# Attention's scores on split operands, keys and queries split in the q stage

## The reference

```python
q = (hn @ w_q).reshape(bsz, L, XATTN_HEADS, XATTN_HEAD_DIM)
k, v = jnp.split(mn @ w_kv, 2, axis=-1)
s = jnp.einsum("blhd,bmhd->bhlm", q, k).astype(jnp.float32) * (XATTN_HEAD_DIM ** -0.5)
p = jax.nn.softmax(s, axis=-1).astype(v.dtype)
o = jnp.einsum("bhlm,bmhd->blhd", p, v).reshape(bsz, L, D_MODEL)
return o @ w_xo
```

## Time and profile before

| | us |
|---|---|
| median of 3 runs | 2433.53 (2432.92 to 2438.96) |
| the profiled execution's own time | 2435.23 |
| its span, first to last instruction | 2433.5 |
| PE (TensorE) busy | 2408.2, 99% |
| PEld (weight loads) busy | 2185.0, 90% |
| DVE (VectorE) busy | 1642.0, 67% |
| ACT (ScalarE) busy | 771.1, 32% |
| POOL (GpSimd) busy | 256.3, 11% |

### The profile page before, as it was taken

How to read it: one execution, slowest core, us unless ns; L and a number is a source line. 1 busy time by engine, 2 the same in 40 slices (tenths; PEclk the granted TensorE clock), 3 DMA queues, 4 the chain that set the end, 5 groups by cost and what they waited for, 6 DMA issues and landing times.

```text
span 2433.5 us, 34372 instructions
## 1 busy us (share of the span) xinstructions
PE 2408.2 (99%) x12524; PEld 2185.0 (90%) x12524; DVE 1642.0 (67%) x3028; ACT 771.1 (32%) x1277; POOL 256.3 (11%) x263
## 2 busy tenths in 40 slices
PE   8999999999999999999999999999999999999998
PEld 6788887788889888888889999999999999999997
DVE  7735453578883884262474687888888788777776
ACT  6401110322223431130352253433333343333333
POOL 0088860000000220000000000001001000000000
PEclk9999999999999999999999999999999999999999
DMA  7532227742227542213332122233232622222222
GB/s 248 162 135 89 77 80 127 209 126 78 73 86 212 207 186 78 95 50 122 114 113 87 44 70 69 83 102 103 91 106 100 257 79 68 76 76 83 76 76 76
DMA packets 121662, 267.25 MB, mean 110 GB/s; under 512 B 15552, under 2 KB 67264, under 8 KB 121536
## 3 DMA queue, kind: packets, MB, share of 16 engines
q1 hardware_dynamic: 113552, 239.85, 31.0%
q0 software_dynamic: 6688, 22.55, 2.5%
q10 hardware_dynamic: 1296, 3.17, 0.4%
HBM read 200.55 MB, written 67.08 MB: 110 GB/s over the span
## 4 chain that ended last, share of the span: by engine, by line
PE 93%; DVE 3%; ACT 1%; DMA 1%; issue 1%; SPq 0%; DVEq 0%; ACTq 0%
PE bank L816 30%; PE bank L818 30%; PE bank L817 30%; PE bank L1062 1%; ACT PB L1570 1%; DVE ON L1827 1%; DVE PT L1827 1%; PE bank L1057 0%; DVE PB L2311 0%; PE bank L1009 0%; DVE smx L2303 0%; PE bank L1016 0%; DMA scratch_KV<-KVS 0%; DMA MEM<-memT 0%; ACT ON L1310 0%
## 5 line engine op out<-in xcount | busy, mean ns | idle before, releaser
L816 PE MATMUL bank<-XN,WLO 128*128 128x512 f32 x1200 | 468.7, 391 | 0.6 <-issue 0.6
L817 PE MATMUL bank<-XN,WHI 128*128 128x512 f32 x1200 | 467.8, 390 | 0.0
L818 PE MATMUL bank<-XN,WHI 128*128 128x512 f32 x1200 | 467.8, 390 | 0.0
L816 PE MATMUL bank<-XH,EL 128*128 128x384 f32 x1232 | 412.8, 335 | 0.0
L817 PE MATMUL bank<-XL,EH 128*128 128x384 f32 x1232 | 412.2, 335 | 0.0
L818 PE MATMUL bank<-XH,EH 128*128 128x384 f32 x1232 | 412.2, 335 | 0.0
L816 PEld LDWEIGHTS bank<-XN,WLO 128*128 128x128 f32 x1200 | 225.4, 188 | 48.8 <-issue 1.8
L817 PEld LDWEIGHTS bank<-XN,WHI 128*128 128x128 f32 x1200 | 225.4, 188 | 47.1 <-issue 0.5
L818 PEld LDWEIGHTS bank<-XN,WHI 128*128 128x128 f32 x1200 | 225.4, 188 | 46.7
L816 PE MATMUL bank<-AF,EL 128*128 128x384 f32 (+2 forms) x704 | 237.0, 337 | 0.5 <-DVE HR L2465 0.3
L817 PE MATMUL bank<-AF,EH 128*128 128x384 f32 (+2 forms) x704 | 235.9, 335 | 0.0
(11 more groups left out here) (295 smaller groups left out, 3760.7 us busy)
## 6 DMA issues: line engine op xcount, KB each, us to landing
RAW<-W_all SPq DMA_DIRECT2D x131, 512.0 KB, 3.6
WR<-W_all SPq DMA_DIRECT2D x92, 512.0 KB, 4.6
scratch_G<-GS SPq DMA_DIRECT2D x16, 768.0 KB, 3.8
scratch_VW<-TB POOLq DMA_DIRECT2D x16, 544.0 KB, 3.4
XS<-xT SPq DMA_DIRECT2D x8, 768.0 KB, 6.0
scratch_CO<-COS SPq DMA_DIRECT2D x8, 768.0 KB, 5.9
COL<-scratch_CO SPq DMA_DIRECT2D x8, 768.0 KB, 4.3
G2L<-scratch_G SPq DMA_DIRECT2D x8, 768.0 KB, 5.8
```

What stands on the lines that cost most here:

```text
L816: pe_mm(out, w[1], x[0], start=first, stop=False, skip_group_check=onto)
L817: pe_mm(out, w[0], x[1], start=False, stop=False, skip_group_check=onto)
L818: return pe_mm(out, w[0], x[0], start=False, stop=last, skip_group_check=onto)
```

## The change

Scores are computed with `product`, from split queries and split keys. The splitting is done once, in the q stage. For each slot j: SyncE loads key tile j (`KF`), ScalarE copies its high part (`KH`), VectorE makes the rest (`KT_LO`), SyncE stores both. Each block of queries goes from PSUM to `QF`, a single buffer (VectorE), to `QH` (ScalarE), to `QT` (VectorE), and SyncE stores both as separate tensors. ScalarE's high part of the next weights (`hi`) stands behind the slot's three copies of queries. In attention the loads of queries and keys are doubled, keys are loaded per head and group. The last slot of the q stage is that of `last_pair`. ScalarE and SyncE wait for all stores of queries before softmax(0) and before `QL` of round 2. The order of work on each engine in a round is as before.

```diff
--- before.py
+++ after.py
@@ -206,18 +206,20 @@
     SQ2 = at("SQ2", 48, [2, T])
     ACC2 = at("ACC2", 82, [T])
     NT = at("NT", 88, [BLK])
-    QS = at("QS", 66, [2, T])
+    QF, QH, QT = at("QF", 64, [BLK]), at("QH", 66, [2, BLK], F32R), at("QT", 70, [2, BLK], F32R)
+    KF, KH, KT_LO = at("KF", 74, [M2]), at("KH", 76, [M2], F32R), at("KT_LO", 78, [M2], F32R)
     XR = at("XR", 66, [2, T])
-    KL = at("KL", 48, [2, 2, M2])
+    KL = at("KL", 48, [2, 2, 2, NMEM], F32R)
     VU = at("VU", 56, [2, 2, 2, 2, P], F32R)
     PB = at("PB", 64, [2, 4, NMEM])
     PT = at("PT", 72, [2, 2, BLK], F32R)
-    QL = at("QL", 80, [2, 2, BLK])
+    QL = [[at("QL00", 80, [2, BLK], F32R), at("QL01", 84, [2, BLK], F32R)], [at("QL10", 88, [2, BLK], F32R)]]
 
     def low(name, kb, shape, dt=F32):
 
         return nc.alloc_sbuf_tensor_at(name, [P] + shape, dt, offset=base + int(kb * K))
 
+    QL[1].append(low("QL11", 18, [2, BLK], F32R))
     YL = low("YL", 0, [HT, C, NC])
     WO += [low(f"WO{q}", S5B_KB[q], [QUAD, 2, P]) for q in range(1, GROUPS // QUAD)]
     ML += [low(f"ML{q}", S5B_KB[q] + 4, [QUAD, P]) for q in range(2, GROUPS // QUAD)]
@@ -253,7 +255,8 @@
     U_d, CO_d, G_d, BB_d, L_d, M_d, Y_d, KV_d, Q_d = (
         scratch[k] for k in ("U", "CO", "G", "BB", "L", "M", "Y", "KV", "Q"))
     W_d = nc.dram_tensor("scratch_VW", (P, GROUPS, 2 * (ROW + GP)), F32).ap()
-    K_d = KV_d[0:KT]
+    K_d = [KV_d[0:KT]] + [nc.dram_tensor(f"scratch_K{n}", (KT, P, M2), F32).ap() for n in range(2)]
+    QQ_d = [Q_d, nc.dram_tensor("scratch_QR", (KT, P, T), F32).ap()]
     VV_d = [v.rearrange("e p (m d) -> e p m d", d=P) for v in
             (KV_d[KT:2 * KT], nc.dram_tensor("scratch_VR", (KT, P, M2), F32).ap())]
 
@@ -576,16 +579,32 @@
         with loop(nc.sync, 3) as i:
             wo(i, True)
         wo(3, False)
-        def queries(i):
-            for par in range(2):
-                weights(SLOT0["q"] + par + 2, par, i)
-                sp.wait_ge(evac, RES0["q"] + NB * (par + 1) + 2 * NB * i)
-                sp.dma_start(tile_of(Q_d, 2 * i + par), QS[:, par, :]).then_inc(S(f"q_stored{par}"), 16)
-
-        def load_memory(h):
-
-            sp.dma_start(KL[:, h % 2], K_d[2 * h:2 * h + 2].rearrange("e p m -> p e m")
-                         ).then_inc(S(f"memory_in{h % 2}"), 16)
+        def keys_load(j):
+
+            sp.dma_start(KF[:], K_d[0][j]).then_inc(S("memory_in0"), 16)
+
+        def keys_store(j):
+
+            sp.wait_ge(S("x_lo"), KT + 4 * j + 1)
+            for to, part in zip(K_d[1:], (KH, KT_LO)):
+                sp.dma_start(to[j], part[:].bitcast(F32)).then_inc(S(f"kv_stored{j % 2}"), 16)
+
+        def queries_store(j):
+
+            for b in range(NB):
+                n = NB * j + b
+                sp.wait_ge(S("x_lo"), KT + 4 * j + b + 2)
+                for to, part in zip(QQ_d, (QH, QT)):
+                    sp.dma_start(to[j][:, blk(b)], part[:, n % 2, :].bitcast(F32)
+                                 ).then_inc(S(f"q_stored{n % 2}"), 16)
+
+        def load_keys(u):
+
+            h, m = u // 2, slice(u % 2 * NMEM, (u % 2 + 1) * NMEM)
+            for part in range(2):
+                sp.dma_start(KL[:, u % 2, part].bitcast(F32),
+                             K_d[1 + part][2 * h:2 * h + 2, :, m].rearrange("e p m -> p e m")
+                             ).then_inc(S(f"memory_in{u % 2}"), 16)
 
         def load_values(u):
 
@@ -597,30 +616,43 @@
 
         def load_queries(n):
             h, b = divmod(n, NB)
-            sp.dma_start(QL[:, n % 2], Q_d[2 * h:2 * h + 2, :, blk(b)].rearrange("e p t -> p e t")
-                         ).then_inc(S(f"queries_in{n % 2}"), 16)
-
-        queries(0)
-
+            for part in range(2):
+                sp.dma_start(QL[n % 2][part][:].bitcast(F32),
+                             QQ_d[part][2 * h:2 * h + 2, :, blk(b)].rearrange("e p t -> p e t")
+                             ).then_inc(S(f"queries_in{n % 2}"), 16)
+
+        sp.wait_ge(evac, RES0["q"])
         for par in range(2):
             sp.wait_ge(S(f"kv_stored{par}"), 192)
-            sp.wait_ge(S(f"q_stored{par}"), 16)
-        for n in range(2):
-            load_memory(n)
-            load_values(n)
-        sp.wait_ge(S("rms"), 2 * NB)
-        for n in range(2):
-            load_queries(n)
-        with nc.sync.Fori(1, 4) as i:
-            queries(i)
+        keys_load(0)
+        for j in range(KT):
+            weights(SLOT0["q"] + j + 2, j % 2)
+            keys_store(j)
+            if j + 1 < KT:
+                keys_load(j + 1)
+            if j == 2:
+                for u in range(2):
+                    load_values(u)
+                for par in range(2):
+                    sp.wait_ge(S(f"q_stored{par}"), 96)
+                sp.wait_ge(S("rms"), 2 * NB)
+                load_queries(0)
+            if j == KT - 1:
+                for par in range(2):
+                    sp.wait_ge(S(f"kv_stored{par}"), 192 + 16 * KT)
+                for u in range(2):
+                    load_keys(u)
+                sp.wait_ge(S("xn_free"), KT + 4)
+                load_queries(1)
+            queries_store(j)
         for par in range(2):
-            sp.wait_ge(S(f"q_stored{par}"), 64)
+            sp.wait_ge(S(f"q_stored{par}"), 16 * NB * KT)
         for n in range(2, HEADS * NB):
             h, b = divmod(n, NB)
             sp.wait_ge(S("scores"), 2 * (n - 1))
             load_queries(n)
-            if b == 1 and 1 <= h < HEADS - 1:
-                load_memory(h + 1)
+            if n - 2 in LAST_ROUND[:-2]:
+                load_keys(LAST_ROUND.index(n - 2) + 2)
             if n - 4 in LAST_ROUND[:-2]:
                 sp.wait_ge(S("att_out"), 2 * (n - 3))
                 load_values(LAST_ROUND.index(n - 4) + 2)
@@ -1072,7 +1104,8 @@
         slots("wo", 3, K8, xin, first=1)
         last_pair("wo", 1)
         first_pair("q", lambda k: (S("hn_lo"), k + 1), 1)
-        slots("q", 4, K8, xin, first=1)
+        slots("q", 3, K8, xin, first=1)
+        last_pair("q", None)
 
 
         pe.wait_ge(evac, RES0["xo"] - NB)
@@ -1081,16 +1114,17 @@
             h, b = divmod(n, NB)
             if n == 1:
                 pe.wait_ge(evac, RES0["xo"])
-            par, mem = n % 2, slice(b * BLK // T_PROMPT * NMEM, (b * BLK // T_PROMPT + 1) * NMEM)
-            pe.wait_ge(S(f"queries_in{par}"), 16 * (n // 2 + 1))
-            pe.wait_ge(S(f"memory_in{h % 2}"), 16 * (h // 2 + 1))
+            par, u = n % 2, 2 * h + b * BLK // T_PROMPT
+            pe.wait_ge(S(f"queries_in{par}"), 32 * (n // 2 + 1))
+            pe.wait_ge(S(f"memory_in{u % 2}"), 32 * (u // 2 + 1) + (1 - u % 2) * 16 * KT)
             if n >= 2:
                 pe.wait_ge(S("exps"), 4 * (n - 1))
             for lt in range(4):
                 out = PS[2 * par + lt // 2][:, (lt % 2) * NMEM:(lt % 2 + 1) * NMEM]
                 for k in range(2):
-                    last = nc.tensor.matmul(out, QL[:, par, k, lt * P:(lt + 1) * P], KL[:, h % 2, k, mem],
-                                            start=k == 0, stop=k == 1)
+                    cols = slice(lt * P, (lt + 1) * P)
+                    last = product(out, (QL[par][0][:, k, cols], QL[par][1][:, k, cols]),
+                                   (KL[:, u % 2, 0, k, :], KL[:, u % 2, 1, k, :]), k == 0, k == 1)
                 if lt % 2:
                     last.then_inc(S("scores"), 1)
 
@@ -1553,14 +1587,24 @@
 
         residual("wo", 1)
         split_residual("wo", 1)
-        hi_pair("q", 0, NB, 1)
-        with nc.scalar.Fori(1, 4) as i:
-            for par in range(2):
-                hi_pair("q", i, NB, par)
-
+        for j in range(KT):
+            act.wait_ge(S("memory_in0"), 16 * (j + 1))
+            if j:
+                act.wait_ge(S(f"kv_stored{(j - 1) % 2}"), 192 + 32 * ((j - 1) // 2 + 1))
+            copy(KH[:], KF[:]).then_inc(S("x_hi"), 1)
+            for b in range(NB):
+                n = NB * j + b
+                act.wait_ge(evac, RES0["q"] + n + 1)
+                if n >= 2:
+                    act.wait_ge(S(f"q_stored{n % 2}"), 32 * (n // 2))
+                copy(QH[:, n % 2, :], QF[:]).then_inc(S("x_hi"), 1)
+            if j + 1 < KT:
+                hi(SLOT0["q"] + j + 2, RES0["q"] + NB * (j + 1))
 
         nc.scalar.activation(rcol[:, 0:1], epsc[:], ACT.Exp)
-        act.wait_ge(S("q_stored0"), 64)
+        for par in range(2):
+            act.wait_ge(S(f"q_stored{par}"), 16 * NB * KT)
+            act.wait_ge(S(f"kv_stored{par}"), 192 + 16 * KT)
 
         def softmax(n):
             par = n % 2
@@ -1581,8 +1625,6 @@
                 act.wait_ge(S("att_out"), 2 * n)
             for m in range(2):
                 act.wait_ge(S("p_turned"), 2 * n + m + 1)
-                if n == m == 0:
-                    act.wait_ge(S("q_stored1"), 64)
                 copy(PT[:, 0, m, :], PS[4 + m][:]).then_inc(S("pt_hi"), 1)
             if n + 2 < HEADS * NB:
                 softmax(n + 2)
@@ -2280,19 +2322,20 @@
```

(27 more changed lines are left out.)

## The result

Median after 2441.08 us (10 runs, 2440.29 to 2444.33), before 2433.48 (10 runs, 2432.55 to 2438.96). The ratio is 1.0033 [1.0025, 1.0041], 6.1 to 10.0 us slower. The forecast was 2440.4. The profiled execution of after has a span of 2439.7 us at a mean granted clock of 0.997, against 2433.5 at 0.999.

The account below looks back on a forecast made before the run. TensorE holds 93% of the chain, but a ScalarE-VectorE ring sets attention's rounds. Losses of 1.6 + 4.6 + 0.7 = 6.9 us on 2433.53 gave 2440.4 us, range 2436.5 to 2446.

Parts of the forecast that it names:

- The forecast case: Whole kernel: three losses in the q stage and at attention's start, rounds unchanged; +6.9 us, 2440.4 us, chance 0.72.
- The third slot: Q stage, third slot: TensorE waits for WLO, made only after slot 0's three query blocks are split; 1.6 us.
- The entry: From q stage to attention: the first exponentials wait for the last split queries' stores; first reciprocal 4.6 us later.
- Cold scores: Attention, scores of round 2: clock halved after TensorE's pause, so second maxima and weighted values come 0.7 us later.
- The rounds at 0: Attention rounds: TensorE's 0.6 us saving per round becomes a wait for PT, so 0 us is gained.
- rounds speed up: Rival, attention: TensorE leads the rounds, so ten are 0.57 us shorter each; 2434.7 us, chance 0.06.
- Weight loads pace the scores: Rival, attention: weight loads cannot come closer than 0.19 us, scores take 4.5 us; 2450 us, chance 0.05.
- transfers lead: Rival, attention: DMA gives 200 GB/s instead of 319 and sets the rounds; +14 us more, 2454, chance 0.08.
- waits half: Rival, q stage and attention's start: faster hand-overs or earlier stores leave only 2 to 3 us; 2436, chance 0.09.
- term 2: Start of attention: waiting for the last split queries' stores makes the first reciprocal 4.6 us later.
- the ring: Attention rounds: ScalarE and VectorE steps wait on each other in a circle without TensorE, 7.04 us a round.

Follow-up runs that it names:

- The kernel with a warm clock: After plus five float32 matmuls of 512 columns into an unused bank after scores(1), filling TensorE's pause: 2441.38 us, 1.0032 of before.
- the order changed: After, with VectorE scaling the probabilities of round n+1 between the maxima of n+2 and the output's rest: 2435.20 us, 1.0005 of before.
- the new order alone: Before, float32 scores kept, with VectorE scaling the probabilities of round n+1 between the maxima of n+2 and the output's rest: 2432.22 us, 0.9992 of before.
- filler: After with one product of high parts for the scores, plus twelve idle 256-column matmuls in each of ten rounds: 2441.85 us, 1.0037 of before.
- the kernel with its own buffer: After with split-query buffers moved, round 2's queries loaded early and a separate buffer for the last block's split queries: 2439.60 us, 1.0021 of before.
- the kernel with all edits and two buffers: After with early weights, moved buffers, early queries and exponential table, VectorE's new order, last block's own buffer, second QF: 2430.45 us, 0.9984 of before.

## Why the prediction was right

The forecast case held: its three terms stand where it put them, and the rounds stayed. All three sizes owe something to luck, as said below.

- *The third slot*, 1.6 forecast, 1.8 measured: `WLO` started 7.7 us after the norm's end (forecast 7.6), the wait is 1.53. It left out the two-buffer wait (0.35 us at the third copy); hand-overs of 0.03 to 0.04 instead of 0.05, and a `WHI` that started 0.09 before the copy's end, made up for it. That is luck. The 1.8 is a start 1.7 late (N + 9.02 after, N + 7.33 before) and 0.1 more until the next matmul.
- *The entry*, 4.6 forecast, 4.6 measured: last rest L + 5.5 (5.64), second store L + 5.95 (6.03), exponentials L + 8.5 (8.49), reciprocal L + 10.45 (10.45). The store took 2.46 from its issue to ScalarE's start; the line through the earlier trace rows gives 2.1 for it, and the forecast's 2.5 was set above it by judgement. That after's profile meets 10.45 to the hundredth is chance: the same stretch took up to 11.15 in the other six profiles. The Trainium skill (*DMA: Bandwidth & Descriptors*, the section with the two cost components of a transfer) gives an estimate of 2.6; it states its figures for transfers that GpSimd issues, these are SyncE's, and 2.46 is near it all the same.
- *Cold scores*, 0.7 forecast, 0.8 measured: the clock came back 5.4 to 5.6 us after 1198.73, as from the start of the kernel. The transposes also ran at half rate, which the forecast left out, so they end at about L + 13.6 and not L + 12.9; the first score starts at L + 13.67, where the forecast had it wait for the queries until L + 14.0. So 17 scores and not 15 were slow, and they end at L + 18.3, as forecast. The step from there to 0.7 isn't worked out in the forecast: its own positions make the second maxima 0.4 us late (L + 18.3 against L + 17.9). They were 0.62 late, and the rest came through the weighted values. The kernel with a warm clock shows that the clock is the cause.
- *The rounds at 0*: right, and for the reason given. TensorE's wait for PT is 0.17 to 0.45 us in the rows and 0.5 in load spacing, forecast 0.6. The scores are 0.119 apart, forecast 0.12. The loads are hidden even at rounds of 6.5.
- *The rivals*: "rounds speed up" needed VectorE's order as well; 6.50 instead of 7.07 is just what it would have given. "Weight loads pace the scores" is out by the spacing, "transfers lead" by the rounds with the order changed, "waits half" by the exact stretches.

The median moved by 7.6 and the three stretches of one trace by 7.2; the forecast's 6.9 lies 0.7 below the median, inside the interval of 6.1 to 10.0, and a term 2 of 4.9 would close half of that.

## What to carry to other kernels

Before pricing a faster operation, find the ring that sets the round: if none of its rows is in it, the saving becomes a wait, and only an edit of the ring turns it into time (here the new order alone was worth 2.0 us in before, hardly clear of noise, the split scores alone nothing in the rounds, the order on top of them 6.6 us). What precomputation costs is to be looked for where its chain has no work beside it, at the first slot and at the hand-over to the next stage: write out multiply, copy, rest, store and load there with their buffers, and ask of each buffer when its own store lets it go. And look at what stands next in the queue: most of what was removed at this entry came back as a wait for the next transfer.

## What the runs showed of the hardware

- A fp32r matmul of 256 columns starts 0.119 us after the last one, with a new weight load each time; float32 scores of the same shapes took 3.5 us a round against 2.86 for three products.
- Less work on TensorE was slower here: without two of three products each round has a wait of about 2 us, and once in the profile the clock (granted 1.00, then 0.50 in the row of 1222.00) falls, after the matmuls have resumed. With filler it doesn't; the mean clock is higher in every execution and the median 3.9 us lower.
- The clock fell in a pause of 2.53 us too (granted 0.55 from 1197.00 to 1200.00 in the kernel with its own buffer), so to shorten the entry's pause from 4.66 us was not enough to keep it. It stayed at 1.00 from 1190.00 to 1200.00 in the kernel with all edits and two buffers, around waits of 2.15 and 1.15 us.
- A wait in TensorE's row understates the loss: 1.53 us in the bracket, 1.8 from start to start.
- Within one kernel fp32r matmuls of 512 columns start 0.227 us apart in most stages and 0.233 in others, in before and after alike. The cause is open.
